# Recurrences of two mixers: the chunks' triangular inverses built two at a time

## The reference

```python
def step(S, inp):                       # RWKV-7, per head, 64 x 64 state
    sa = jnp.einsum('bhij,bhj->bhi', S, at)
    S = S * wt[:, :, None, :] + sa[..., None] * bt[:, :, None, :] + vt[..., None] * kt[:, :, None, :]
    return S, jnp.einsum('bhij,bhj->bhi', S, rt)
...
sol = lax.linalg.triangular_solve(jnp.eye(C, dtype=jnp.float32) + lower, rhs,   # gated delta rule
                                  left_side=True, lower=True, unit_diagonal=True)
```

## Time and profile before

| | us |
|---|---|
| median of 3 runs (lowest, highest) | 3484.43 (3483.56, 3487.03) |
| the profiled execution | 3478.72 |
| its span, first to last instruction | 3476.9 |
| mean granted clock of TensorE | 0.981 |
| first recurrence, first step of substitution to last output | 632.1 to 754.7 |
| second recurrence, the same | 1784.7 to 1907.7 |

### The profile page before, as it was taken

How to read it: one execution, slowest core, us unless ns; L and a number is a source line. 1 busy time by engine, 2 the same in 40 slices (tenths; PEclk the granted TensorE clock), 3 DMA queues, 4 the chain that set the end, 5 groups by cost and what they waited for, 6 DMA issues and landing times.

```text
span 3476.9 us, 47334 instructions
## 1 busy us (share of the span) xinstructions
PE 3358.7 (97%) x16932; PEld 2760.2 (79%) x16932; DVE 1424.3 (41%) x2739; ACT 1267.1 (36%) x1976; POOL 1675.9 (48%) x2052
## 2 busy tenths in 40 slices
PE   7999998899999999999989999999899999999999
PEld 6888776788888888887668888878667888888887
DVE  5431598855221322148786522123663110441100
ACT  4222436534222322234563422232533332433321
POOL 6765542006665566655400466645304555435554
PEclk9999999799999999999979999999999999999999
DMA  5443321003443344333100344332102222212222
GB/s 186 145 145 109 109 91 56 13 19 133 145 144 110 127 145 145 121 103 98 61 25 1 109 145 145 127 104 82 58 1 91 97 97 97 85 61 97 97 97 97
DMA packets 104225, 340.51 MB, mean 98 GB/s; under 512 B 12144, under 2 KB 17936, under 8 KB 103968
## 3 DMA queue, kind: packets, MB, share of 16 engines
q1 hardware_dynamic: 87824, 283.08, 24.6%
q10 hardware_dynamic: 16272, 55.65, 4.8%
HBM read 330.78 MB, written 2.65 MB: 96 GB/s over the span
## 4 chain that ended last, share of the span: by engine, by line
issue 38%; POOL 33%; PE 27%; DVE 1%; POOLq 0%; ACT 0%; DVEq 0%
POOL w_lo L721 33%; PE ps L2313 7%; PE ps L2314 7%; PE ps L2315 7%; PE ps L3094 1%; PE ps L2336 0%; PE ps L3073 0%; PE ps L2337 0%; PE ps L2341 0%; PE ps L3082 0%; PE ps L3184 0%; DVE stat L2214 0%; DVE sq L2207 0%; PE ps L3190 0%; PE ps L3074 0%
## 5 line engine op out<-in xcount | busy, mean ns | idle before, releaser
L721 POOL TENSOR_TENSOR w_lo<-w_raw,w_hi 128x256 fp32r<-128x256 f32 x2040 | 1669.2, 850 | 1783.3 <-ACT w_hi L764 1776.1
L2313 PE MATMUL ps<-h_hi,w_hi 128*128 128x512 f32 x2608 | 1019.9, 391 | 0.9 <-ACT mem L981 0.9
L2315 PE MATMUL ps<-h_hi,w_lo 128*128 128x512 f32 x2608 | 1015.7, 389 | 0.0
L2314 PE MATMUL ps<-h_lo,w_hi 128*128 128x512 f32 x2608 | 1015.6, 389 | 0.0
L764 ACT ACTIVATE w_hi<-w_raw 128x1024 fp32r<-128x1024 f32 x510 | 538.2, 1057 | 927.2 <-DMA w_raw<-in_tiles 927.0
L2313 PEld LDWEIGHTS ps<-h_hi,w_hi 128*128 128x128 f32 x2608 | 490.0, 188 | 113.3 <-issue 6.4
L2315 PEld LDWEIGHTS ps<-h_hi,w_lo 128*128 128x128 f32 x2608 | 490.0, 188 | 102.9
L2314 PEld LDWEIGHTS ps<-h_lo,w_hi 128*128 128x128 f32 x2608 | 490.0, 188 | 100.3
L2314 PE MATMUL ps<-a_lo,w_hi 128*128 (+1 forms) x1120 | 435.8, 389 | 0.0
L2313 PE MATMUL ps<-a_hi,w_hi 128*128 (+1 forms) x1056 | 410.8, 389 | 0.0
L2315 PE MATMUL ps<-a_hi,w_lo 128*128 (+1 forms) x1056 | 410.8, 389 | 0.0
(11 more groups left out here) (477 smaller groups left out, 3589.4 us busy)
## 6 DMA issues: line engine op xcount, KB each, us to landing
w_raw<-in_tiles SPq DMA_DIRECT2D x510, 512.0 KB, 3.3
ada_raw<-in_ada_tiles ACTq DMA_DIRECT2D x96, 512.0 KB, 3.3
mem<-mem SPq DMA_DIRECT2D x80, 64.0 KB, 2.1
x<-in_x_t SPq DMA_DIRECT2D x2, 1024.0 KB, 6.6
sq<-in_cond ACTq DMA_DIRECT2D x4, 512.0 KB, 4.2
mem<-gates SPq DMA_DIRECT2D x8, 256.0 KB, 3.9
consts<-in_consts SPq DMA_DIRECT2D x1, 1280.0 KB, 12.8
core_mem<-gates SPq DMA_DIRECT2D x8, 128.0 KB, 2.9
```

The costliest lines, as they stand in the source:

```text
L721: ins = nc.gpsimd.tensor_tensor(w_lo[:, s, part], w_raw[:, s, part], w_hi[:, s, part].bitcast(F32), ALU.subtract)
L2313: nc.tensor.matmul(bank, wh, hi, start=first, stop=False, skip_group_check=True)
L2314: nc.tensor.matmul(bank, wh, lo, start=False, stop=False, skip_group_check=True)
L2315: return nc.tensor.matmul(bank, wl, hi, start=False, stop=last, skip_group_check=True)
```

## The change

Chunks are paired, (0, 1) and (2, 3).

- One substitution serves a pair: buffers have 16 heads, the mask and the fresh identity are for 256 columns, `spread_inverses` places four units after one transpose of 512 columns.
- Level 4: `lower_corners`, its mask and its buffer go. The first product uses L itself, 64 columns wide, and VectorE masks it on the way out (`mask_products`), in place of ScalarE's copy. Only the increment of the plain form is a product; the transposed form is made by VectorE's 32 x 32 transpose after the addition.
- A pair is merged in banks 2 to 5; first and second products of a chunk share a bank, in its two halves.
- The order is written out for pairs, in one function `core` for each engine. TensorE: level 4 of both chunks, level 5 of both, level 6 of the even one, and then the two recurrences, with level 6 of the odd one inside the first. VectorE: the substitution of pair (2, 3) is cut into 6, 5 and 4 steps, with the masks and states of the first pair's recurrences between them. Chunk 1's grams are taken before the first substitution.
- There are two states in turn, the outputs of both recurrences share bank 7 and come after the state's products; ScalarE's six plain and two scaled turn-outs come ahead of two of the decays; one DMA of constants goes.

```diff
+                substitute(range(15, 0, -1))
+                spread_inverses(l, 0)
+                fresh_rows()
+                mask_products(0)
+                mask_products(1)
+                take_a_grams(0, (0, 1))
+                merge16(0)
+                V.tensor_tensor(mem[:, 37:39, :], mem[:, U_QG:U_QG + 2, :], mem[:, 41:43, :], ALU.mult)
+                V.scalar_tensor_tensor(mem[:, 24:26, :], mem[:, 39:41, :], -1.0, mem[:, 41:43, :], ALU.mult, ALU.mult).then_inc(S["gdn_ready"], 1)
+                merge16(1)
...
+                def merge16(n):
+
+                    for g in range(2):
+                        inv, inv_t = inv_units(n)[:, g, :], inv_t_units(n)[:, g, :]
+                        dve.wait_ge(S["dx_ready"], merge_turn(TB * l + n, 4, g) + 1)
+                        link(V.tensor_tensor(evens(inv, 4), evens(inv, 4), compact(ps[:, merge_bank(n, g), half[0]], 4), ALU.add))
+                        V.transpose(inv_t, inv).then_inc(S["merged16"], 1)
...
+                for even in (0, 2):
+                    odd, n = even + 1, even + 1
...
+                    lower_products(even, 4)
+                    lower_products(odd, 4)
+                    inverse_products(even, 4)
+                    inverse_products(odd, 4)
+                    if even:
+                        pe.wait_ge(S["s_out"], TB * l + even + 1)
+                        pe.wait_ge(S["y_out"], TB * l + even)
+                        a_grams(even, (0, 1))
...
+                    lower_products(even, 5)
+                    lower_products(odd, 5)
+                    inverse_products(even, 5)
+                    inverse_products(odd, 5)
...
+                    lower_products(even, 6)
+                    inverse_products(even, 6)
+                    right_sides(n)
+                    lower_products(odd, 6)
+                    writes(n)
+                    a_grams(odd, (0,))
+                    inverse_products(odd, 6)
+                    state_products(n)
+                    outputs(n)
+                    pe.wait_ge(S["merged64"], 2 * (TB * l + odd) + 2)
+                    a_grams(odd, (1,))
+                    right_sides(n + 1)
+                    writes(n + 1)
+                    state_products(n + 1)
+                    outputs(n + 1)
```

More of the change, by code:

```diff
@@ L598, in _ @@
         def _(sp):
-            first, last = 2 * P, CONST_AT["eps"]
+            first, last, small = 2 * P, CONST_AT["sel_pair"], CONST_AT["eps"]
             half = KD // 2
@@ new lines, in core @@
+                merge16(1)
+                dve.wait_ge(S["eg_ready"], 4 * l + 4)
+                take_grams(l, 2)
+                small_blocks(l, 2)
+                take_a_grams(0, (2, 3))
+                take_grams(l, 3)
+                small_blocks(l, 3)
+                substitute(range(15, 9, -1))
+                take_a_grams(1, (0, 1))
+                next_state(1)
+                take_a_grams(1, (2, 3))
+                substitute(range(9, 4, -1))
+                next_state(2)
+                substitute(range(4, 0, -1))
@@ new lines, in core @@
+                spread_inverses(l, 2)
+                mask_products(2)
+                mask_products(3)
+                merge16(2)
+                take_a_grams(2, range(4))
+                merge16(3)
+                take_a_grams(3, (0, 1))
+                next_state(3)
+                take_a_grams(3, (2, 3))
+                for k in range(4):
+                    dve.wait_ge(S["h_hi_ready"], due("h_hi_ready"))
+                    V.tensor_tensor(attended_lo[:, k, :], mem[:, U_Y + k, :], attended_hi[:, k, :].bitcast(F32), ALU.subtract).then_inc(S["h_ready"], 1)
@@ L2703, in recurrences @@
                     turn(src, turn_bank(n))
-                pe.wait_ge(S["turned_out"], seen["turn"])
-                for n in range(TB + 1):
-                    core_step(l, n)
+                core(l)
                 post(l)
@@ L2762, in inverse_products, with lower_products @@
-                def inverse_products(lev, g):
-                    pe.wait_ge(S["t1_out"], merge_turn(b, lev, g) + 1)
+                slot = lambda ru, hh, j: ru[:, P * j + HD * hh:P * j + HD * hh + HD]
+                def lower_products(n, lev):
+                    b = TB * l + n
+                    for g in range(2):
+                        pe.wait_ge(S[{4: "small_ready", 5: "merged16", 6: "merged32"}[lev]], 2 * b + g + 1)
+                        first = {4: 0, 5: 32, 6: HD}[lev]
+                        rows = slice(HD, P) if lev == 6 else slice(0, P - first)
+                        for h in range(4):
+                            inv = inv_units(n)[:, g, blk(h)]
+                            out = ps[rows, merge_bank(n, g), HD * h:HD * h + HD]
+                            ins = nc.tensor.matmul(compact(out, lev), lower_units(n)[:, g, P * h + first:P * h + P], evens(inv, lev), start=True, stop=True)
+                        ins.then_inc(S["t1_ready"], 1)
@@ L2795, in right_sides, with a_grams @@
+                def a_grams(n, kinds):
+                    for kind in kinds:
+                        pairs = ((kt, ap), (kt, rt)) if kind == 0 else ((nb, rt), (kg, qg))
+                        grams([a_banks(n, 2 * kind + hh) for hh in range(2)], "a_gram_ready", pairs, n)
+                def right_sides(n):
+                    b, last = TB * l + n, n - 1
                     if n == 1:
@@ L2839, in outputs @@
+                def outputs(n):
+                    b, last = TB * l + n, n - 1
+                    tm = lambda u, hh: mem[:, u, last * P + HD * hh:last * P + HD * hh + HD]
+                    pe.wait_ge(S["a_gram_out"], 4 * b)
+                    if n > 1:
+                        pe.wait_ge(S["y_out"], b - 1)
+                    for c in range(2):
+                        nc.tensor.matmul(ps[:, 7, blk(c)], state_of(n)[:, c, :], rt(c)[:, blk(last)], start=True, stop=False)
                         for hh in range(2):
@@ L2864, in core_step @@
[L2864 to L2874 removed]
+                pe.wait_ge(S["gram_taken"], 2 * TB * l + 4)
```

421 lines of the change are left out of this document (179 added, 242 removed).

## The result

The changed kernel takes **3529.5 us** in the median of 4 runs (3503.8 to 3539.7), the kernel before 3484.0 (3479.3 to 3487.0) on the same chip: 1.012 of before, with an interval of 1.0086 to 1.0155. It is slower, as forecast, but the forecast was 3504 and its range ended at 3522: the time lies outside. The four runs of the changed kernel differ by 36 us where those of before differ by 8; that turned out to be part of the finding.

What follows compares the result with a forecast made beforehand. VectorE bounds the recurrences' first half, the chain through TensorE and ScalarE the rest. Per layer -3.9 path, +9.1 and +4 clock, 1 for the first pair: +10; two layers +20 on 3484.4 give 3504, range 3474 to 3522.

Steps and rivals of the forecast that it cites:

- (a): Start of the first pair: substitution starts later, at 636.3, and ends at 654.8; TensorE's first product at 654.0.
- (b): First pair, TensorE's first product to right sides 1: 22.6 us, so 676.6.
- (c): First pair's two recurrences with level 6 of chunk 1 inside: 22.3 us, TensorE stopping at 698.9.
- (d): Before the second pair: last four substitution steps and the tail end at 705.8, leaving TensorE idle 6.9 us.
- (e): Second pair up to right sides 3: 23.1 us at the full clock, so 729.0; before, the same point is at 729.45.
- +9.1: Second pair at half clock after the idling: level 4's eight groups 7.6 us more, the grams behind them 1.5.
- The row from 662 to 664: Profile row of chunk 0's levels 5 and 6: clock 0.50 though TensorE is busy 2.00 of 2.00 us; the forecast followed it.
- (f): The two last recurrences: 21.8 us, ending at 750.8 in place of 754.7.
- -3.9 a layer: Recurrence path at the full clock: 3.9 us less a layer, all that stays of VectorE's 17 us.
- +14: Clock loss a layer: 9.1 in second-pair level 4 and grams, 4 in levels 5 and 6, 1 in the first pair.
- Rival 3: Half clock holds longer: both pairs run levels 4 to 6 cold, with right sides and writes; +19 a layer, 3522; chance 0.15.
- VectorE's relief: VectorE in the recurrences: some 17 us less work a layer, mainly from one substitution serving a pair.

Runs made afterwards that it cites:

- e7: e3 and e6 together on the changed kernel, plus three 128 x 128 idle products at ScalarE's copies in each pair's second recurrence; 3491.4 us, 1.002 of before.
- e3: Changed kernel with the whole second substitution before the first recurrence's grams are masked, and chunk 3's lower grams earlier; 3500.7 us, 1.0045 of before.
- e5: Changed kernel with six idle products filling TensorE's pause before the second pair's level 4; 3512.4 us, 1.0078 of before.
- e13: e5 with both level 4 merges ahead of VectorE's grams in the second pair, and the `gdn_ready` work behind both merges in the first; 3489.3 us, 1.0004.
- e6: Changed kernel with idle products only ahead of the first pair: four before the last two turns, two before the first grams; 3506.6 us, 1.0062 of before.
- e2: e1 plus idle products between the groups of levels 5 and 6 and at ScalarE's copies in each pair's second recurrence; 3531.3 us, 1.0136 of before.
- e10: e7 with `gdn_ready` work behind both merges, two level orders mended, one idle product less, half the second pair's first grams between its level 5s; 3478.1 us, 0.9987.
- e12: e7 with `gdn_ready` work behind both merges, two level orders mended, one idle product less, last three second-substitution steps behind the first state; 3467.5 us, 0.9962.
- e1: Changed kernel with 12 idle products of 128 x 512 on TensorE in the pause before the second pair's level 4; 3525.0 us, 1.0113 of before.
- e14: e12 without any idle product, so the order of real work alone; 3471.8 us, 0.9963 of before.
- e4: Changed kernel with the second pair's first grams moved from behind level 4 into the pause ahead of it; 3505.3 us, 1.0069 of before.
- e11: e3 with `gdn_ready` work behind both merges and two level orders mended, without any idle product; 3487.7 us, 1.0008 of before.

## Why the prediction was wrong, step by step

Measured in the first layer of the changed kernel, from its first mark.

**(a) Right.** Level 4 begins 37.7 us behind the mark (655.0); predicted were 38.8.

**(b) Right in its order, wrong in the clock.** 22.6 us predicted to right sides 1. With no half clock it took 23.6 in e7's second layer (chunk 3's grams stand earlier there). In the changed kernel it was 26.9 in one layer (0.81) and 35.7 in the other (0.54). For this I had allowed 1 us a layer; it was 3.3 and 12.1.

**(c) Too short by 2.** 22.3 predicted until TensorE stops, 24.4 measured (681.9 to 706.3, full clock).

**(d) Right.** 6.9 us of pause predicted, 5.94 measured; e3 and e5 show cause and place.

**(e) Right in size, in part by luck.** 23.1 at the full clock, and 9.1 and a mean of 4 for the half: measured 36.1 in both layers, 13 over. The +9.1 behind the pause stands by e5. The part in levels 5 and 6 was the middle of 0 and 8, one layer of the two; it came in both layers (13.7 us at 0.50 in each) at about half the price, and that the two errors cancel is luck. What decides it the prediction did not say. The row from 662 to 664 shows products that *began* at the half clock, behind a pause of 1.27 us. And the wait for VectorE's masks ahead of level 5, which I had counted as a delay alone (2 us; 0.99 measured, 1.51 in e5), was the cause here: e13 takes it away, and the same products run at 1.00.

**(f) Too short by 2, and a clock term missed.** 21.8 predicted to ScalarE's last output, 26.5 measured (748.4 to 774.9). The last outputs took 6.3 us where those of chunk 2 took 3.6, at the half clock, and it was still at 0.77 in the mixing: from the means to the mixing's second `head_spread` products it took 15.5 us in both layers, before 12.7 and 13.0. That is 2.9 and 2.6 of the 4.8 and 3.9 us behind the recurrences; what lies behind the second one differs by 5 us among the profiles without this half clock too, so the rest is no more than scatter. Before, grams of the last chunk stood in the first of ScalarE's two copies there; the change had done them earlier. But the two pauses of 0.69 us that this leaves are not enough by themselves: e5, e6 and e13 have them too and ran that stretch at 1.00. It fell in 7 of 18 such stretches of the profiled executions without idle products there, and in none of 12 with them (e2, e7 to e10, e12).

At the full clock the steps were off by -1.1 + 1.0 + 2.1 - 0.9 + 2.0 = 3.1, which makes the forecast's -3.9 a layer **-0.8**. The clock, for which I took +14, is 3.3 + 13.0 + 2.7 = **19.0** in the first layer: together 18.2, and at ScalarE's last output 18.1 are measured (157.6 us behind the mark, 139.5 before). In the second layer the first pair adds 9 more. The failing term is the clock of the first pair and of the end (1 us allowed a layer, 6.0 and 14.8 measured), not that of the second pair's level 4; the -3.9 of the path, which was -0.8, is the second. Rival 3 (the half clock in both pairs, +19 a layer, chance 0.15) is nearest to what came. Its mechanism came in part: right sides and writes ran at 1.00, and so did the first layer's first level 4, while the second layer's first pair and the mixing cost more than it had. All this is the profiled execution, the slowest. The median is 16 us lower, and how those executions divide isn't shown.

The rule of the Trainium skill that I had set against the row (TensorE: Matmul & The Clock Gate, Part 1: sustained matmul activity releases the clock) is borne out in part only: in row 3 of e13 matmuls ran unbroken (35.39 of 35.90 us busy, 0.54), and the half clock held for 33 us of them before it ended. What I came to hold in e1's theory B, that narrow work drops the clock, is not borne out by rows 1, 2 and 4.

The scatter fits this. One long half clock in a first pair is worth some 14 us (34.8 us in place of 21.3 in e14, whose two groups lie 12 us apart, with mean clocks of 0.982 to 0.984 and 0.978 to 0.979). The changed kernel's best run, 3503.8, has a mean clock of 0.976 and its two worst 0.966; the fourth (3521.6, 0.923) doesn't fit, and I can't say why.

**Left open:** why the 3.8 us of grams ahead of level 4 lift the clock in one layer and not in the other, from the same instructions after the same pauses; and why it ended in level 6 and not in levels 4 and 5. In the profiled executions with no idle product ahead of the first pair and none in it (the changed kernel, e1, e3, e4, e5, e11, e13, e14) it stayed down for 30 us or more in no first layer of eight and in seven second layers of eight; with idle products ahead (e6 to e10, e12) in one layer of twelve. That the moment at which the burst comes decides it is argued from this, not shown. How much of VectorE's relief the transposes in place of a product give alone was not tried.

## What to carry to other kernels

When work is regrouped so that two engines take turns instead of overlapping, price each new pause on TensorE twice: its own length, and what runs behind it at half the clock until it rises again. Here pauses of 1 to 6 us cost another 4 to 9 us in the narrow products after them, and the cure is to order the waits of the *other* engines (masks before or after merges, the last steps of a serial loop behind the state), not to add work: here idle products paid only in a pause that was there anyway. And when a row shows work at a low clock, look at what the clock was when that work began before calling the work the cause.

## What was unexpected of the hardware

- The same 225 records of level 4 to right sides 1 took 20.9 us and 35.9 us within one execution (e13), with TensorE busy in all but 0.5 us of either: the clock rose 0.5 us behind their start in the one, 33 us behind it in the other.
- In e4 the half clock lasted for 27 us in which TensorE was busy all the time (714 to 741), and ended with no product wider than 64 columns since 712.5.
- An idle product of 128 x 512 in f32 takes 0.88 us at the full clock (24 records, 12 products, 10.57 us).
